# One macaron layer on one Trainium2 core: the first feed-forward block is split in two phases, context alone, then latents with seven products for eight

## The reference, cut to what matters

```python
m_x = jnp.split(jax.nn.silu(c) @ w_ada[l] + b_ada[l], 9, axis=-1)      # w_ada: 1024 x 9216
m_c = jnp.split(jax.nn.silu(c_ctx) @ w_ada[l] + b_ada[l], 9, axis=-1)

def swiglu(h, w1, w2):                       # w1: 1024 x 5632, w2: 2816 x 1024
    gate, up = jnp.split(h @ w1, 2, axis=-1)
    return (jax.nn.silu(gate) * up) @ w2

x   = x   + 0.5 * m_x[2] * swiglu(modulate(rmsnorm(x, g0),   m_x[0], m_x[1]), ffn1_w1, ffn1_w2)
ctx = ctx + 0.5 * m_c[2] * swiglu(modulate(rmsnorm(ctx, g0), m_c[0], m_c[1]), ffn1_w1, ffn1_w2)
...   # mixer: retention heads and chunk gMLP on modulate(rmsnorm(.), m[3], m[4]) @ w_in, then @ w_out
x = x + 0.5 * m_x[8] * swiglu(modulate(rmsnorm(x, g2), m_x[6], m_x[7]), ffn2_w1, ffn2_w2)
return rmsnorm(x, final_g)
```

## Time and profile before

| what | value |
|---|---|
| median of 3 runs | 2205.12 us |
| profiled execution | 2204.2 us, span 2202.4 us |
| PE busy | 2141.5 us (97%) |
| DVE busy | 1306.7 us (59%) |
| POOL busy | 659.7 us (30%) |
| ACT busy | 544.7 us (25%) |
| first feed-forward block, 11 iterations | 926.1 us |
| mean granted TensorE clock | 0.989 of 2.4 GHz |

### The profile page before, as it was taken

How to read it: one execution, slowest core, us unless ns; L and a number is a source line. 1 busy time by engine, 2 the same in 40 slices (tenths; PEclk the granted TensorE clock), 3 DMA queues, 4 the chain that set the end, 5 groups by cost and what they waited for, 6 DMA issues and landing times.

```text
span 2202.4 us, 28857 instructions
## 1 busy us (share of the span) xinstructions
PE 2141.5 (97%) x10960; PEld 1798.5 (82%) x10960; DVE 1306.7 (59%) x1997; ACT 544.7 (25%) x819; POOL 659.7 (30%) x340
## 2 busy tenths in 40 slices
PE   8899999999999999998999999998899999999997
PEld 3688888888888888887788899876788888888886
DVE  4754454454454454468725345469677777777767
ACT  3311111111111111124320211335232332222222
POOL 1611111111111121115422213464343443344431
PEclk9999999999999999999999999999999999999998
DMA  9112111111111211113101021220101111101112
GB/s 355 68 48 90 53 48 69 74 48 67 76 48 67 76 48 67 58 58 112 52 16 58 20 87 39 77 100 16 58 31 55 57 57 57 52 33 57 57 39 77
DMA packets 28378, 144.43 MB, mean 66 GB/s; under 512 B 3361, under 2 KB 4641, under 8 KB 15009
## 3 DMA queue, kind: packets, MB, share of 16 engines
q1 hardware_dynamic: 28320, 143.64, 17.6%
HBM read 139.44 MB, written 4.19 MB: 65 GB/s over the span
## 4 chain that ended last, share of the span: by engine, by line
PE 88%; DVE 6%; ACT 1%; issue 1%; POOL 1%; DMA 1%; SPq 0%; DVEq 0%; ACTq 0%; POOLq 0%
PE PS L1593 22%; PE PS L1595 22%; PE PS L1594 22%; PE PS L1846 6%; PE PS L1847 6%; PE PS L1848 6%; PE PS L1639 1%; PE PS L1630 1%; POOL HL L537 1%; PE PS L1788 1%; DVE DG L1033 1%; DMA X<-x 1%; DVE HF L1055 1%; DMA WR<-w_units 1%; DVE ACC L1020 1%
## 5 line engine op out<-in xcount | busy, mean ns | idle before, releaser
L1593 PE MATMUL PS<-HH,WH 128*128 128x512 f32 x1088 | 426.9, 392 | 5.2 <-POOL HL L537 3.3
L1595 PE MATMUL PS<-HH,WL 128*128 128x512 f32 x1088 | 424.1, 390 | 0.0
L1594 PE MATMUL PS<-HL,WH 128*128 128x512 f32 x1088 | 424.0, 390 | 0.0
L520 POOL TENSOR_TENSOR WL<-WR,WH 128x2048 fp32r<-128x2048 f32 x42 | 193.4, 4606 | 535.2 <-ACT WH L673 535.1
L1461 DVE SCALAR_TENSOR_TENSOR X<-PS,GATE,X 128x512 f32<-128x512 f32 x352 | 242.4, 745 | 89.8 <-PE PS L1595 89.7
L1593 PEld LDWEIGHTS PS<-HH,WH 128*128 128x128 f32 x1088 | 204.7, 188 | 48.2 <-issue 4.4
L1595 PEld LDWEIGHTS PS<-HH,WL 128*128 128x128 f32 x1088 | 204.5, 188 | 42.9
L1594 PEld LDWEIGHTS PS<-HL,WH 128*128 128x128 f32 x1088 | 204.8, 188 | 41.9 <-issue 0.7
L1178 DVE TENSOR_TENSOR PR<-SG,PS 128x512 f32<-128x512 f32 (+1 forms) x66 | 39.5, 599 | 296.7 <-ACT SG L725 291.4
L1194 DVE SCALAR_TENSOR_TENSOR X<-PS,GATE,X 128x512 f32<-128x512 f32 x176 | 132.1, 751 | 108.0 <-PE PS L1595 108.0
L725 ACT ACTIVATE SG<-PS 128x512 f32<-128x512 f32 (+1 forms) x66 | 34.5, 523 | 639.6 <-PE PS L1595 639.6
(11 more groups left out here) (247 smaller groups left out, 4219.8 us busy)
## 6 DMA issues: line engine op xcount, KB each, us to landing
WR<-w_units SPq DMA_DIRECT2D x91, 1024.0 KB, 5.3
W2R<-w_units SPq DMA_DIRECT2D x44, 512.0 KB, 3.6
WS<-ada_units SPq DMA_DIRECT2D x12, 1024.0 KB, 7.7
X<-x SPq DMA_DIRECT2D x2, 2048.0 KB, 14.1
out<-OUT SPq DMA_DIRECT2D x2, 1024.0 KB, 4.2
out<-OUT SPq DMA_DIRECT2D x3, 512.0 KB, 4.1
XC<-ctx SPq DMA_DIRECT2D x1, 1024.0 KB, 5.5
RAW<-w_units SPq DMA_DIRECT2D x1, 1024.0 KB, 6.8
```

The source lines that it names most:

```text
L520: pool.tensor_tensor(WL[:, slot], WR[:, slot], WH[:, slot].bitcast(F32), ALU.subtract).then_inc(s_lo[slot], 1)
L1593: pe.matmul(dst, wh, xh, start=first, stop=False)
L1594: pe.matmul(dst, wh, xl, start=False, stop=False)
L1595: return pe.matmul(dst, wl, xh, start=False, stop=last)
```

## The change

The first feed-forward block becomes two phases.

- **Context phase.** 22 units one by one, for the 256 context tokens only: 48 matmuls of 256 columns for gate and up, then 24 for the down product of the unit before. The down products of all units add up in PSUM (four banks), so they are added to the context once, at the end. The low part of `w1` (`WL`, 128 x 2048) is made on GpSimd, that of `w2` (`W2LB`, 128 x 1024) on DVE. Eight units of `w_ada` go through TensorE before it, twelve as sums on DVE inside it (24 sums early, then 12 per unit). The latents are loaded in it, and their norm, their modulation and their high and low parts are made in its last ten units.
- **Latent phase.** The function `feed_forward(f)` now serves both blocks: the seven products, with all of `w1` and `w2` loaded a second time for the first block. The context is scaled for its mixer norm at the start of the phase, stored to DRAM and loaded back at the end.
- **Mixer.** The last 16 units of `w_ada`, for latents only (8 sums each on DVE), each pass through the buffer of the weight unit that is loaded next: unit i is loaded after the sums of the `w_ada` unit before it in the same buffer have been reduced on TensorE.
- The second block's first units take their parts in another order (`ORDER1`).

The core of the diff (the second block's functions move into `feed_forward(f)` with few changes; they are left out):

```diff
+FIRST_UNITS = NF + 1
+ADA_PE, ADA_CTX = 8, 20
+ADA_EARLY = 24
+ADA_STEP = 12
+MIX_FIRST, MIX_LAST = 4, 19
...
+def ada_sums_done(p):
+    return min(ADA_EARLY + ADA_STEP * (p + 1), 180 + 6 * max(0, p - 12), 16 * (ADA_CTX - ADA_PE)) if p >= 0 else ADA_EARLY
...
 # SP
+            for p in range(NF):
+                b = p + 3
+                if b < FIRST_UNITS:
+                    sp.wait_ge(s_lo[(b + 1) % 2], (p + 1) // 2 + 1)
+                    unit(first_source(b % NF), (b + 1) % 2)
+                if p + 1 < NF:
+                    sp.wait_ge(s_w2lo, p + 1)
+                    sp.dma_start(W2RB[:, :], w2_units[p + 1]).then_inc(s_w2raw, 16)
...
+            for i in range(2, len(MIX_UNITS)):
+                sp.wait_ge(s_lo[i % 2], unit_count(i - 2))
+                if MIX_FIRST <= i - 2 <= MIX_LAST:
+                    a = ada_after(i - 2)
+                    sp.dma_start(WR[:, i % 2], ada_source(a)).then_inc(s_first[a % 8], 16)
+                    sp.wait_ge(s_col, a + 1)
+                unit(w_units[mix_unit(i)], i % 2)
...
 # POOL
+            for b in range(2, FIRST_UNITS):
+                unit_low((b + 1) % 2, b + 1)
+                if b in (16, 18):
+                    norm_rsqrt(0, 1 if b == 16 else 2)
+            feed_forward(0)
...
 # ACT
+            for p in range(NF):
+                if p:
+                    down_high(p - 1)
+                if 1 <= p < FIRST_UNITS - 1:
+                    act.wait_ge(s_gu, p)
+                    high(p % 2, 16 * ((p + 1) // 2 + 1))
+                act.wait_ge(s_gu, p + 1)
+                if p:
+                    act.wait_ge(s_prod, p)
+                act.activation(SG[:, :], PS[p % 2][:, 0:CTX], ACT.Silu).then_inc(s_silu, 1)
+                act.wait_ge(s_prod, p + 1)
+                if p >= 2:
+                    act.wait_ge(s_yb, p - 1)
+                act.activation(PH[:, p % 2, :], PR[:, :], ACT.Copy).then_inc(s_ph, 1)
+                if 12 <= p < 16:
+                    ...   # four squares of the latents
+                if p in (16, 17, 19, 20):
+                    ...   # four modulations, four high parts of the latents
...
 # DVE
+            for p in range(NF):
+                if p:
+                    down_low(p - 1)
+                ...   # modulation vectors of the units whose sums are reduced
+                for n in range(ada_sums_done(p - 1), ada_sums_done(p)):
+                    ada_sum(n)
+                ...   # p 13 to 21: squares added, norm, scaling, low parts of the latents
+                dve.wait_ge(s_silu, p + 1)
+                if p:
+                    dve.wait_ge(s_pl, p)
+                dve.tensor_tensor(PR[:, :], SG[:, :], PS[p % 2][:, CTX:2 * CTX], ALU.mult).then_inc(s_prod, 1)
+                ctx_low(p)
+            down_low(NF - 1)
...
 # PE
+            for p in range(NF):
+                ctx_gate_up(p)
+                if p:
+                    ctx_down(p - 1)
...
+                if n == FIRST_FILL[i]:
+                    if MIX_FIRST < i <= MIX_LAST + 1:
+                        latent_columns(ada_after(i - 1), 1 - slot)
+                    pe.wait_ge(s_lo[slot], unit_count(i))
```

More of the change, by code:

```diff
@@ L1 @@
+from collections import namedtuple
 from contextlib import ExitStack
@@ new lines, in _ @@
+            for k in range(KT):
+                act.wait_ge(s_hf, 8 * J[1, 0] + k + 1)
+                act.activation(HCH[:, k, :], XC[:, k, :], ACT.Copy).then_inc(s_hh, 1)
+            act.wait_ge(BS[0].dl, NF)
+            act.wait_ge(BS[0].c12, NF - 1)
+            act.wait_ge(BS[0].c22, NF - 1)
+            high(0, 16 * unit_count(0))
+            act.wait_ge(BS[0].m[6], NF)
+            for k in range(KT):
+                act.wait_ge(BS[0].fyd, NYB + 16 * (NF - 1) + k + 1)
+                square(1, 1, k)
@@ L850, in _ @@
+            act.wait_ge(BS[0].fy, 16 * (NF - 1))
+            high(1, 16 * unit_count(1))
+            for k in range(KT):
+                act.wait_ge(BS[0].fyd, NYB + 16 * (NF - 1) + KT + k + 1)
+                square(1, 2, k)
             mix_high(2)
@@ new lines, in ctx_down @@
+            def ctx_down(p):
+                pe.wait_ge(s_pl, p + 1)
+                pe.wait_ge(s_w2lo, p + 1)
+                for d in range(KT):
+                    dst = PS[2 + d // 2][:, d % 2 * CTX:(d % 2 + 1) * CTX]
+                    w, last = slice(d * P, (d + 1) * P), p == NF - 1
+                    pe.matmul(dst, W2HB[:, w], PH[:, p % 2, :], start=p == 0 and d % 2 == 0, stop=False, skip_group_check=True)
+                    pe.matmul(dst, W2HB[:, w], PL[:, p % 2, :], start=False, stop=False, skip_group_check=True)
+                    ins = pe.matmul(dst, W2LB[:, w], PH[:, p % 2, :], start=False, stop=last, skip_group_check=True)
+                ins.then_inc(s_yb, 1)
@@ new lines, in square_sum, with last_norm @@
+            def square_sum(t, k, first=False):
+                if k:
+                    pe.wait_ge(s_sqt, KT * t + k + 1)
+                else:
+                    pe.wait_ge(s_qt[t], 3)
+                for c in range(4):
+                    ins = pe.matmul(ST_BANK[:, c:c + 1], SQT[:, 8 * t + k, c * P:(c + 1) * P], ONES[:, 0:1],
+                                    start=first and c == 0, stop=False, skip_group_check=True)
+                return ins
+            def last_norm(d):
+                if d == 1:
+                    pe.wait_ge(s_ms, J[3, 1])
+                    square_sum(0, 4, first=True)
+                    square_sum(0, 5)
+                if d == 3:
+                    square_sum(0, 6)
+                    square_sum(0, 7)
+                if d == 5:
+                    square_sum(0, 0).then_inc(s_st, 1)
```

1859 lines of the change are left out of this document (991 added, 868 removed).

## The result

The changed kernel takes 2289.38 us (median of 4 runs, 2286.11 to 2294.32) against 2205.26 us of the kernel before: ratio 1.038, 95% interval 1.0363 to 1.0397. It is slower by 84 us. The forecast was 2250 us with a range of 2182 to 2285: the direction is right, the size is not, and the time lies 4 us above the range.

The account below looks back on a forecast made before the run. TensorE's issue pace was taken to bound the kernel. Block +31, entry to the mixer -1 and mixer +15 make +45 on the profiled 2204.2, thus 2249; the runs' median stands 0.9 higher: 2250 us, range 2182 to 2285 (8 in 10).

Parts of the forecast that it names:

- first `PR`: Start of the context phase: the first gated product stands at 65 us, behind the early modulation units, sums and low parts.
- units 1 to 12: Ordinary context units: TensorE needs 8.2 us, but VectorE's chain with GpSimd's 4.6 inside takes 12.5 each, 150 us.
- units 13 to 21: Late context units, with latent work on ACT and VectorE added: 15.3 us and more each, 134 us together.
- context to latents: Passage in the first block: 40 us from the last gated product of the context until TensorE starts the latents' main work.
- TensorE's rest of the block: Latent phase of the first block: 2820 matmuls of 512 columns and 0.28 us a unit, 646 us.
- into the mixer: Block's end: about 9 us wait for VectorE, against context work covering norms; together -1 us, bounds -8 and +10.
- The first rival: VectorE and GpSimd do not exclude each other, or VectorE's waits lie beside TensorE's work: 2166 us, chance 0.17.
- GpSimd waits for the sums to end: Context phase: GpSimd's low part starts only behind VectorE's sums, 1.5 us less in each of 12 units: 2232 us, chance 0.15.
- the third rival: TensorE's clock falls in the context phase's gaps, a unit at 1.2 GHz takes 15.3 us: 2284 us, chance 0.06.
- The mixer hides all: Rival for the mixer: its added modulation work costs no time: 2235 us, chance 0.10.
- 38 us more of sums hide: Mixer's latent units: VectorE, busy 186 of 391 us, takes 38 us more of modulation sums at no cost.
- 3.4 us per output unit: Mixer's output units: TensorE waits for sums pushed to 14.0 us; four units at 3.4, one at 1.4: 15 us, bounds 0 and 25.

## Why the prediction was wrong, point by point

| Term | Predicted | Measured |
|---|---|---|
| first `PR` | 65 | 65.08 |
| units 1 to 12 | 12.5 each, 150 | 11.9 each, 143.0 |
| units 13 to 21 | 134 | 126.7 |
| context to latents | 40 | 40, set |
| TensorE's rest of the block | 646 | 647, to 1022 (687 with the 40) |
| block against before | +31 | +17.7 |
| into the mixer | -1 (-8 to +10) | +19.5 |
| k, q and latent units | 0 | +18.1 |
| output units | +15 (0 to 25) | +30.6 |
| sum | +45 | +85.9 |

**The mechanism of the context phase was right.** VectorE and GpSimd exclude each other, the unit is VectorE's chain, and seven products for eight is paid only where TensorE is the bound. The first rival ("not excluded", 2166) falls by the run with the low parts on VectorE. "GpSimd waits for the sums to end" falls by the row of 8.35 us. The clock was 0.93 and 0.88 in the context phase; the third rival's drop through whole units did not come. "The mixer hides all" falls by the run without the pass.

**The context phase was over-estimated** by 14 us. I had added all parts as if each stood whole; measured, ten sums grow by 4.3 where GpSimd's row is 4.8, twelve with it take 8.8 where I had 9.4, and what stands ahead of the sums is 3.06 for 3.25. This error hid part of the others, so the total looks better than its terms, which is luck. A slip at the start did not show: eight modulation units at 4.2 us from 6.3 us end near 40 and not 43, and the first `PR` came at 65.08 all the same.

**The step that failed first is "Into the mixer".** I saw the 9 us that VectorE's additions would cost, but I counted three things wrong: of GpSimd's instructions I set one low part into VectorE's row, and there are two (5.02 for 0.68 and 3.63 for 0.42 us, 7.5 us together); ACT makes 8.5 us of context tokens and a weight's high part ahead of the first square, for which VectorE waits 3.5; and the 10 us that I set against it, for the context products, did not come, since the norm's chain starts only behind the last additions. The clock was 0.72 there. The rows show these three; no run takes them apart, and the one with the other order gave back 6 to 7 of the 19.5 us.

**The second is "38 us more of sums hide" in the latent units.** The argument was a mean over the stretch (21.8 us of TensorE per weight load, VectorE under half busy). The k and q units are shorter than this mean, their ropes fill VectorE's row, and TensorE's first columns waited 7.5 us for sums behind the second rope. The columns themselves, 0.5 us each, were counted at nothing.

**The third is the mis-sized 3.4 us per output unit.** I let the modulation unit's data be there in time (5.3 us behind its own issue) and counted one round of 12.2 and the sums to 14.0. Measured, the last three rounds take 17.1 us each. Missing were two things that only together could be mended. The queue: the load stands behind a wait for the unit before and behind the next weights, so it arrives just when GpSimd starts. And the place: an X addition and a square's addition stand ahead of the sums, and the latter stands still until GpSimd ends. So the sums do not lie beside the load and GpSimd's low part but behind them, with 4.0 us for eight where I had 3.2. That TensorE's waits for the sums add up to 15.2 us here, just the 15 forecast, is luck: about 13 more are lost at half clock (an estimate: half of the 26 us with a clock of 0.50, a matmul of 512 columns every 0.43 us for 0.227), for which the mixer had no term, and 2 are the columns.

**The range** took the unknown costs of the terms that had bounds. The latent units had none and cost 18 us, and three terms failed to the same side. In two of them GpSimd made VectorE's row longer than counted.

## What to carry to other kernels

Before moving an elementwise step to an idle GpSimd, look at what VectorE does at that moment: if it works on SBUF alone, the step costs about GpSimd's longer time in VectorE's row (the rows show it for two SBUF inputs, and for a sum and a copy that read one tensor), and VectorE's own 2.3 us would have been cheaper than GpSimd's 4.6. A fixed order on a DMA queue is part of the loop: draw one round with issue, landing, high part, low part and sums on a line before saying that something hides. Two edits that are each worth next to nothing can be worth 15 us together, when one gives the data and the other the place. Compare runs of different sets by their ratios, or at a row of the trace behind which nothing was edited.

## What the runs showed of the hardware

- Ten `scalar_tensor_tensor` of 256 columns take 4.04 us alone and 8.35 with a GpSimd subtraction of 4.79 us begun 0.1 us behind the first; a GpSimd instruction of 0.96 us made ten of them 4.52. A single short one behind GpSimd's start takes what is left of it: 4.38 us for 0.34. This one is a `tensor_scalar` that reads one tensor, and the copy at 1040.39 (3.63 us for 0.42) does so too, so here not only instructions with two SBUF tensors stand still.
- Additions to X with one input in PSUM run at 0.66 us each beside GpSimd's subtractions (19 in 12.60 us), no longer than alone.
- TensorE's granted clock was 0.50 for about 6.5 us behind each of its four waits for the sums in the output units. One of them was 8.1 us long; the others were 2.3, 2.3 and 2.5, with a clock of 1.00 ahead of them. Rows of the kernel after (start, duration), and the stretch behind the second wait:

```profile
1471.58 1.01 PE L1860 MATMUL PS<-ONES,WR 128*128 128x1 f32 x4 [8.08 <-DVE WR L1290]
...
1476.87 0.63 PE L1814 MATMUL PS<-HL,WH 128*128 128x512 f32 x1
1477.29 0.63 PE L1815 MATMUL PS<-HH,WL 128*128 128x512 f32 x1
...
1488.65 1.01 PE L1860 MATMUL PS<-ONES,WR 128*128 128x1 f32 x4 [2.31 <-DVE WR L1290]
...
1488.70:1495.20 6.50, 6.50 (x17) 5.27 (x18) 1.16 (x2) 0.66 (x1) 0.00 (x0) 0.50 0.69 241
```
